# A two-block transformer kernel on one core: rotary exchange by a VectorE shuffle, boundary tiles in PSUM, first loads from two engines

## The chip, the core and the metric

The kernel runs on one core of a Trainium2 chip. The metric is the device time of one launch in microseconds (us), the median of several runs. TensorE multiplies matrices into PSUM; VectorE (DVE), ScalarE (ACT) and GpSimd (POOL) work element by element; SyncE (SP) and ScalarE issue the DMA transfers here. Each engine works off its own instruction stream in order and waits for semaphores of the others.

## What is computed

Two blocks of two layers each on x of 1024 tokens x 1024 columns, in float32. A layer of the first block:

```python
def rotate(x, cos, sin):
    x1, x2 = jnp.split(x, 2, axis=-1)
    return jnp.concatenate([x1 * cos - x2 * sin, x2 * cos + x1 * sin], axis=-1)
...
    h = rms_norm(x, norm_g)
    proj = h @ w_in
    (aq, ak, av, az, cx, cb, cc, cz, rq, rk, rv, rz, gates) = jnp.split(proj, split_points, axis=-1)
    a = diff_attention(aq, ak, av, lam, attn_subln_g, lam_init) * jax.nn.silu(az)
    c = short_conv(cx, cb, cc, conv_w) * jax.nn.silu(cz)
    r = retention(rq, rk, rv) * jax.nn.silu(rz)
    g = jax.nn.sigmoid(gates.astype(jnp.float32)).reshape(b, s, N_BRANCH, D_MODEL)
    merged = g[:, :, 0] * (branches[0] @ w_branch[0])
    ...
    return x + (merged @ w_out).astype(x.dtype)
```

(arguments shortened to what matters). In diff_attention the first 16 of each head's 64 columns of q and k are rotated (two halves of 8 are exchanged and multiplied by the sine); in retention all 64 are (two halves of 32). The first block ends in a further rms_norm. A layer of the second block is again x + y @ w_out, with h = rms_norm(x) ahead of its projection; its y joins a 31-tap convolution, an attention of eight heads and a gated unit, each with a norm of its own.

## The kernel before

Everything is laid out with features on the 128 partitions and tokens along the free axis: X is eight tiles (j) of 128 features x 1024 tokens, worked in two halves of 512 tokens. A product in float32 is made of three: the input is split into a high part (Hhi) and the rest (Hlo), and so is each weight panel (Whi, Wlo, split by GpSimd at L449 and L452 from what SyncE loads at L429); `three_pass` (L502) and `three_pass_half` (L483) issue the 24 matmuls of a half panel. GpSimd splits the next panel once TensorE says `panel_begun`.

All orders are written out by hand, one stream for each engine; nothing is scheduled by a planner. In the first block (`first_block`, L531; TensorE's stream from L688, ScalarE's from L975, VectorE's from L1256) a layer runs: attention over four heads, merge 0, convolution, merge 1, retention in two pairs of heads, merge 2, and 16 output panels OUT (two halves x eight tiles).

The attention of a head has eight queries q of 128 tokens: TensorE's `scores` (L731, with the mask at L736), VectorE's `maxima` (L1274), ScalarE's exponentials (L994), VectorE's `mix` (L1283 to L1285, adds `mixed`), TensorE's transposes of the mixed rows (L709, they wait for `mixed`), and products with the values. TensorE issues the scores of query q+2 before the transposes of q+1. Between the queries the table B1_SLOTS places the pieces of the next head: panel halves `q`, `k`, `v`, `z`, and `sq`/`sk`, a matmul with a permutation matrix (L765, `swapa`) that exchanges the halves of q or k. ScalarE copies the raw panel to SBUF (L1004), TensorE swaps it into another bank of the ring F (three banks), and VectorE multiplies by sine (L1294) and cosine (L1295) and adds (L1297). In retention the same is done over 1024 tokens, with `swapr` at L703.

At a passage between layers VectorE adds each OUT panel to x (L1600; `x_ready`), ScalarE squares it and stores x to the buffer xs, VectorE adds the squares up (`add_out_square`, L1507, and L1512 for the additional norm), TensorE sums them over partitions with a matrix of ones (L684; L673 and L677 in the last layer), ScalarE makes the root (`norm_root`), VectorE scales x (L1452, or L1459 for the second block), ScalarE copies the high part (L1153), VectorE subtracts to get the low one (L1466). The first half of tokens is done during outputs 10 to 15 of the second half, at places that HIGH_AT lists; the second half after the last OUT. OUT uses four banks of PSUM. The second block has the same chain with its own lines (L1770, L2306, L2311, L2429), the MLA branch's `final` scalings and `low` splits among the outputs 3 to 7, and, at its beginning, the panels g and a with the 31 taps on VectorE (L2334), 62 instructions over 1024 columns.

At the start ScalarE issues the loads of x, tables and parameters (L1161, L659 to L664, L1759 to L1761), then squares each of eight token tiles; VectorE scales them (L1435), TensorE turns them (L709), and ScalarE and VectorE split them.

## Time and profile before

| | |
|---|---|
| median of 3 runs | 3921.5 us (3919.44 to 3929.78) |
| the profiled execution | 3918.32 us, its span 3916.4 us |
| TensorE busy | 3709.7 us, 95% |
| VectorE busy | 1857.9 us, 47% |
| GpSimd busy | 1421.8 us, 36% |
| ScalarE busy | 1110.0 us, 28% |
| granted TensorE clock, mean | 0.981 of full speed |

The profile has one row for each group of instructions with their start and length, and behind a row in brackets how long the engine had been idle and which instruction of another engine released it. Idle time of TensorE is what counts first; idle time of the others counts where TensorE waits for them. Matmuls overlap in the pipeline, so the distance between the starts of two rows tells more than a row's length.

### The profile page before, as it was taken

How to read it: one execution, taken by the hardware profiler on the slowest of the kernel's cores; microseconds unless marked ns; L12 is line 12 of the kernel's file. 1: busy time of each engine (PE TensorE's matmuls, PEld its weight loads, DVE VectorE, ACT ScalarE, POOL GpSimd, SP SyncE). 2: the span in 40 equal slices, each digit the busy share in tenths (PEclk: the TensorE clock that was granted, in tenths of full speed). 3: DMA queues.
4: the chain of work that ended last, by engine and by line, in shares of the span. 5: the costliest groups of instructions: out<-in, count | busy, mean ns of one | idle time of the engine just before them, and what ended most of it. 6: DMA issues, size and time to landing. Idle time of an engine off the chain costs nothing.

```text
span 3916.4 us, 43068 instructions
## 1 busy us (share of the span) xinstructions
PE 3709.7 (95%) x16664; PEld 2834.0 (72%) x16664; DVE 1857.9 (47%) x2125; ACT 1110.0 (28%) x1817; POOL 1421.8 (36%) x734
## 2 busy tenths in 40 slices
PE   6989999999999999999999998899899989999998
PEld 5666788887877666788887876777666668766666
DVE  3665113223157555113223148962666589345654
ACT  3334100112212334210112212123465321335542
POOL 1212344432356222344342356433322345333324
PEclk9999999999999999999999998999899989999999
DMA  4000111111133100111111123211111231111122
GB/s 148 28 27 27 51 51 46 44 51 33 36 121 108 33 27 27 46 51 46 48 46 34 40 81 94 93 43 33 33 32 31 94 98 49 33 33 33 32 71 86
DMA packets 75580, 209.40 MB, mean 53 GB/s; under 512 B 9120, under 2 KB 14496, under 8 KB 74912
## 3 DMA queue, kind: packets, MB, share of 16 engines
q1 hardware_dynamic: 52992, 156.98, 13.8%
q10 hardware_dynamic: 22432, 50.18, 3.4%
q8 instruction: 118, 1.93, 0.2%
q14 instruction: 38, 0.31, 0.0%
HBM read 186.16 MB, written 20.97 MB: 53 GB/s over the span
## 4 chain that ended last, share of the span: by engine, by line
PE 85%; DVE 9%; ACT 4%; issue 1%; ACTq 1%; DMA 0%; DVEq 0%
PE psA L502 45%; PE psT L483 16%; PE psA L483 5%; PE psA L1820 3%; PE psA L731 2%; PE psT L1885 2%; PE psT L781 2%; PE psT L1791 1%; PE psT L1796 1%; DVE b_rowmax L1274 1%; DVE Hlo L2311 1%; PE psT L1864 1%; ACT X L994 1%; PE psT L1861 1%; PE psT L703 1%
## 5 line engine op out<-in xcount | busy, mean ns | idle before, releaser
L449 POOL TENSOR_TENSOR Whi<-stage,credit 128x1024 fp32r<-128x1024 f32 (+2 forms) x364 | 605.5, 1664 | 2446.9 <-PE psA L502 1213.2
L452 POOL TENSOR_TENSOR Wlo<-stage,Whi 128x1024 fp32r<-128x1024 f32 (+2 forms) x364 | 815.9, 2242 | 28.5
L502 PE MATMUL psA<-Hhi,Whi 128*128 128x512 f32 x2240 | 703.7, 395 | 11.9 <-ACT b_wk L2054 11.9
L502 PE MATMUL psA<-Hlo,Whi 128*128 128x512 f32 x2240 | 691.1, 390 | 0.0
L502 PE MATMUL psA<-Hhi,Wlo 128*128 128x512 f32 x2240 | 690.8, 390 | 0.0
L502 PEld LDWEIGHTS psA<-Hhi,Whi 128*128 128x128 f32 x2240 | 420.1, 188 | 113.0 <-issue 28.1
L502 PEld LDWEIGHTS psA<-Hlo,Whi 128*128 128x128 f32 x2240 | 421.1, 188 | 88.4
L502 PEld LDWEIGHTS psA<-Hhi,Wlo 128*128 128x128 f32 x2240 | 421.1, 188 | 88.2
L483 PE MATMUL psT<-Hhi,Whi 128*128 128x512 f32 x1024 | 424.8, 415 | 35.0 <-ACT b_upad L1017 18.8
L483 PE MATMUL psT<-Hhi,Wlo 128*128 128x512 f32 x1024 | 404.4, 395 | 0.0
L483 PE MATMUL psT<-Hlo,Whi 128*128 128x512 f32 x1024 | 404.1, 395 | 0.0
L483 PEld LDWEIGHTS psT<-Hhi,Whi 128*128 128x128 f32 x1024 | 196.1, 192 | 92.0 <-issue 52.6
L2334 DVE SCALAR_TENSOR_TENSOR b_wk<-b_ypad,b_cur,b_wk 128x1024 f32<-128x1024 f32 x120 | 227.3, 1895 | 4.1
L483 PEld LDWEIGHTS psT<-Hhi,Wlo 128*128 128x128 f32 x1024 | 195.3, 191 | 43.2
L483 PEld LDWEIGHTS psT<-Hlo,Whi 128*128 128x128 f32 x1024 | 196.2, 192 | 39.1 <-issue 3.4
L483 PE MATMUL psA<-Hhi,Whi 128*128 128x512 f32 x448 | 186.7, 417 | 29.2 <-DVE Hlo L2311 15.3
L483 PE MATMUL psA<-Hlo,Whi 128*128 128x512 f32 x448 | 178.9, 399 | 0.0
L483 PE MATMUL psA<-Hhi,Wlo 128*128 128x512 f32 x448 | 178.4, 398 | 0.0
L1274 DVE TENSOR_REDUCE b_rowmax<-psA 128x1 f32<-128x256 f32 (+7 forms) x128 | 97.0, 757 | 169.4 <-PE psA L736 167.2
L987 ACT ACTIVATE b_wk<-psA 128x1024 f32<-128x1024 f32 x44 | 45.2, 1028 | 443.0 <-PE psA L502 442.9
L1094 ACT ACTIVATE b_wk<-psA 128x1024 f32<-128x1024 f32 x32 | 32.9, 1027 | 440.8 <-PE psA L502 440.8
L1820 PE MATMUL psA<-b_wk 128*128 128x512 f32 (+3 forms) x384 | 149.6, 499 | 5.0 <-ACT b_wk L2075 4.5
(301 smaller groups left out, 4996.9 us busy)
## 6 DMA issues: line engine op xcount, KB each, us to landing
stage<-in_w SPq DMA_DIRECT2D x232, 512.0 KB, 3.5
stage<-in_w SPq DMA_DIRECT2D x68, 256.0 KB, 2.6
xs<-X ACTq DMA_DIRECT2D x64, 256.0 KB, 3.2
stage<-in_w SPq DMA_DIRECT2D x32, 384.0 KB, 3.1
b_wk<-xs ACTq DMA_DIRECT2D x36, 256.0 KB, 4.9
b_wk<-in_x ACTq DMA_DIRECT2D x8, 512.0 KB, 11.3
rope<-in_ropes ACTq DMA_DIRECT2D x4, 1024.0 KB, 7.2
stage<-in_w SPq DMA_DIRECT2D x32, 128.0 KB, 2.1
```

Of the source, the lines that this page charges most:

```text
L449: pool.tensor_tensor(Whi[:, b, 0:n], stage[:, b, 0:n], credit[:, 0:1].broadcast_to([P, n]), ALU.add).then_inc(s.w_hi, 1)
L452: pool.tensor_tensor(Wlo[:, b, 0:n], stage[:, b, 0:n], Whi[:, b, 0:n].bitcast(F32), ALU.subtract).then_inc(s.w_split, 1)
L483: mm = pe.matmul(dst[0:M], w[:, cols], r[k][:, c], start=k == 0 and w is whi and r is rhi, stop=k == nk - 1 and end)
L502: mm = pe.matmul(dst[h], w[:, cols], r[k][:, h * HALF:(h + 1) * HALF], start=first and k == order[0] and r is rhi and w is whi, stop=last ...
L703: mm = pe.matmul(dst[:, c], lhsT, rhs[:, c], start=start, stop=stop)
L731: pe.matmul(dst[:, k0:k1], AQ[h % 2][rows, q * P:n], AK[h % 2][rows, k0:k1], start=True, stop=k1 < n)
L781: mm = pe.matmul(psAV[:, c0:], AVAL[h % 2][:, k * P:(k + 1) * P], WT[:, k, c0:], start=k == 0, stop=k == 4 * g + 3)
L987: act.activation(dst, psA[:, A.buf(use)], func).then_inc(A.freed(use), 1)
L1274: step(dve.reduce_max(rowmax[:, c:c + 1], psA[:, A.buf(use), 0:n], AX_X))
L1820: pe.matmul(dst[:, k0:k1], Q[sd][:, q * P:n], keys[g][:, 0:k1 - k0], start=True, stop=k1 < n)
L1885: mm = pe.matmul(psAV[side_rows(sd), c0:], v[:, b * M_V:(b + 1) * M_V], WT[sd][:, k, c0:], start=k == 0, stop=k == 4 * g + 3)
L2334: ins = dve.scalar_tensor_tensor(out=YC[:, t], in0=ypad[:, t, k:k + SEQ], scalar=col(C2.conv_w + 2 * k + t), in1=YC[:, t], op0=ALU.mult, o ...
```

## The change

Three parts.

1. In the first block the swap matmuls are gone, with the two matrices and ScalarE's copies. VectorE reads the raw panel from PSUM: a stream shuffle with a list of 32 lanes writes the exchanged panel to SBUF, a product takes the raw panel by cosine, and the bank is then free. Retention's columns are permuted on the host (PAIRED), so that its exchange lies within 32 lanes too. `sq` and `sk` are gone from the slots.
2. At the passages the squares, the roots and the scaled tiles lie in PSUM. OUT of the first block uses two banks. The scalings are spread otherwise (NORM_AT, NORM_AT2 in place of HIGH_AT); in the second block the sum comes one output earlier, and `final` is spread over outputs 3 to 6. The last scaling of the first block's output is split: half 0 at outputs 14 and 15, half 1 (`last_finished`) inside the second block, behind its first `glu`. xs is stored by one transfer of 2 MB for each half in place of eight.
3. At the start SyncE issues the first four token tiles, ScalarE only the gains and the other four; rope, parameters and tables come later. The order of turns and panels is another.

The core of the diff:

```diff
-B1_PRELUDE = [("q", 0, 0), ("k", 0, 0), ("sq", 0, 0), ("sk", 0, 0), ("q", 0, 1), ("k", 0, 1), ("sq", 0, 1),
-              ("sk", 0, 1), ("v", 0, 0), ("v", 0, 1)]
+B1_PRELUDE = [("q", 0, 0), ("k", 0, 0), ("q", 0, 1), ("k", 0, 1), ("v", 0, 0), ("v", 0, 1)]
 B1_SLOTS = [([("vt", 0, 0)], [("q", 1, 0), ("x0", 0, 0, True)]),
             ([("vt", 0, 1)], [("q", 1, 1), ("x0", 0, 1, True)]),
-            ([("sq", 1, 0)], [("k", 1, 0), ("b0", 0, 0, True), ("ss", -1, 1)]),
-            ([], [("sq", 1, 1), ("k", 1, 1), ("b0", 0, 1, True)]),
-            ([("sk", 1, 0)], [("z", 0, 0)]),
-            ([("sk", 1, 1)], [("z", 0, 1)]),
+            ([], [("k", 1, 0), ("b0", 0, 0, True), ("ss", -1, 1)]),
+            ([], [("k", 1, 1), ("b0", 0, 1, True)]),
+            ([], [("z", 0, 0)]),
+            ([], [("z", 0, 1)]),
...
+def exchange(half):
+
+    return [i ^ half if i < 2 * half else i for i in range(32)]
+
+
 OUTS = [(half, j) for half in (0, 1) for j in range(KT)]
-HIGH_AT = {10: (0,), 11: (1,), 12: (2, 3), 13: (4,), 14: (5, 6), 15: (7,)}
+NORM_AT = {10: (0, 1), 11: (2, 3), 12: (4, 5), 13: (6, 7)}
+NORM_AT2 = {9: (0,), 10: (1,), 11: (2,), 12: (3,), 13: (4,), 14: (5,), 15: (6, 7)}
...
+        OUT, RSTD, ROOT2 = [psA[:, b, 0:HALF] for b in (0, 1)], psT[:, 1, HALF:], psT[:, 1, 0:HALF]
+        SQ, SQ2, MEAN2, ROOT1 = (psT[:, 1, 0:HALF], psT[:, 0, 0:HALF]), psT[:, 0, HALF:], rraw[:, 0, 0:HALF], rraw[:, 0, HALF:]
+
+        def scaled_tile(L, half, t):
+
+            if L == DEPTH and half:
+                return psT[:, 0, cols(t % 2)]
+            return psA[:, t % 2, HALF:]
...
+            sp.dma_start(ident[:], env.consts[:, K.ident:K.ident + P]).then_inc(consts_in, 16)
+            for t in range(4):
+                sp.dma_start(XT[t], x_tiles[t]).then_inc(x_in[t], 16)
+            for k, dst in ((K.ones, ones[:]), (K.mask, MASK)):
                 sp.dma_start(dst, env.consts[:, k:k + P]).then_inc(consts_in, 16)
...
+                        turn_normed((4, 5))
+                    elif L == 0 and use == ("k", 0, 0):
+                        turn_normed((6, 7))
+                        turn_tokens(0)
+                    elif L == 0 and use == ("q", 0, 1):
+                        turn_tokens(1)
...
-                swap(L, ("swaprq", 0), ("rq", 0), swapr, R_RAWQ)
-                swap(L, ("swaprk", 0), ("rk", 0), swapr, R_RAWK)
...
-                    if n >= 4:
-                        pe.wait_ge(*x_ready.upto(L, n - 3))
-                    elif n % 2 == 0:
-                        pe.wait_ge(*A.drained(L, ("branch", 2, KT - 2 + n // 2)))
-                    three_pass_half(pe, out_bank(psA, n), env.Whi[:, p % 2], env.Wlo[:, p % 2],
+                    if n >= 2:
+                        pe.wait_ge(*x_ready.upto(L, n - 1))
+                    else:
+                        pe.wait_ge(*A.drained(L, ("branch", 2, KT - 2 + n)))
+                    three_pass_half(pe, OUT[n % 2], env.Whi[:, p % 2], env.Wlo[:, p % 2],
...
-                    if L + 1 < DEPTH:
-                        act.dma_start(xs_v[:, j, c], x).then_inc(saved[half].sem, 16)
+                    if L + 1 < DEPTH and j == KT - 1:
+                        act.dma_start(xs_v[:, :, c], X[:, :, c]).then_inc(saved[half].sem, 16)
...
+                step(dve.stream_shuffle(R_ROT, raw, exchange(16)))
+                dve.tensor_tensor(dst, raw, rope[:, 0], ALU.mult).then_inc(A.freed(use), 1)
+                step(dve.tensor_tensor(R_ROT, R_ROT, rope[:, 1], ALU.mult))
+                dve.wait_ge(*A.drained(L, use))
                 dve.tensor_tensor(dst, dst, R_ROT, ALU.add).then_inc(done, 1)
...
+                if kind in ("q", "k"):
+                    dst = (AQ if kind == "q" else AK)[h % 2][:, c]
                     dve.wait_ge(*F.filled(L, use))
-                    dve.tensor_tensor(ROT, psF, rope[:, 1, c], ALU.mult).then_inc(F.freed(use), 1)
-                    step(dve.tensor_tensor(dst, dst, rope[:, 0, c], ALU.mult))
+                    step(dve.stream_shuffle(ROT, psF, exchange(8)))
+                    dve.tensor_tensor(dst, psF, rope[:, 0, c], ALU.mult).then_inc(F.freed(use), 1)
+                    step(dve.tensor_tensor(ROT, ROT, rope[:, 1, c], ALU.mult))
                     dve.wait_ge(*F.drained(L, use))
                     dve.tensor_tensor(dst, dst, ROT, ALU.add).then_inc(rotated.sem, 1)
...
+                if half * KT + t >= 2:
+                    dve.wait_ge(*h_lo.upto(L, half * KT + t - 1))
+                if t == 0:
+                    dve.wait_ge(*((both, half + 1) if L == DEPTH else rstd.upto(L - 1, half + 1)))
+                gain, root = (env.gg, MEAN2) if L == DEPTH else (cur[:, C1.norm:C1.norm + KT], RSTD)
+                dve.scalar_tensor_tensor(out=scaled_tile(L, half, t), in0=X[:, t, cols(half)], scalar=gain[:, t:t + 1],
+                                         in1=root, op0=ALU.mult, op1=ALU.mult).then_inc(h_scaled.sem, 1)
...
+                dve.tensor_tensor(SQSUM[:, c], SQ[L], SQSUM[:, c], ALU.add).then_inc(sq_added.sem, 1)
...
-                    normed(L + 1, 0, HIGH_AT.get(n, ()))
-                    if n == 2 * KT - 2 and L + 1 == DEPTH:
+                    normed(L + 1, 0, NORM_AT.get(n, ()))
+                    if n >= 2 * KT - 2 and L + 1 == DEPTH:
                         for t in range(4):
-                            finished(0, t)
+                            finished(0, n % 2 * 4 + t)
...
+        def last_finished(dve):
+            for j in range(KT):
+                dve.scalar_tensor_tensor(out=X[:, j, cols(1)], in0=X[:, j, cols(1)], scalar=fing[:, j:j + 1], in1=RSTD,
+                                         op0=ALU.mult, op1=ALU.mult).then_inc(x_fin, 1)
...
+        SQ, RSTD, M_ROOT = bank_of((last + 1) % 3), bank_of((last + 2) % 3), psAV
+        HT, MT, OUT_BANKS = [bank_of(last), psAV], [bank_of(last), RSTD], [psA[:, b, cols(h)] for h in (0, 1) for b in (0, 1)]
...
-                        if n == KT + 1:
+                        if n == KT:
...
+                    if 3 <= n < 7:
+                        final(L, 1, n - 3)
+                    if 4 <= n < 8:
                         low(L, 1, n - 4)
```

Three places, as the streams stand. First TensorE in the first head's attention, from the scores of query 4 (512 and 128 columns) to the next panel, before:

```order
L731 MATMUL psA<-b_wk 128x512 [waits b1A1_drained,b1A0_drained]
L731 MATMUL psA<-b_wk 128x512
L731 MATMUL psA<-b_wk 128x128 x2
L736 MATMUL psA<-maskb,identb 128x128 x2
L709 MATMUL psT<-ident,X 128x128 [waits b1F1_drained,b1_mixed]
L709 MATMUL psT<-ident,X 128x128 x3
L765 MATMUL psT<-b_wk,b_swapa 128x512 [waits b1F2_drained,b1F0_drained]
```

and with the change:

```order
L720 MATMUL psA<-b_wk 128x512 [waits b1A1_drained,b1A0_drained]
L720 MATMUL psA<-b_wk 128x512
L720 MATMUL psA<-b_wk 128x128 x2
L725 MATMUL psA<-maskb,identb 128x128 x2
L704 MATMUL psT<-ident,X 128x128 [waits b1F2_drained,b1_mixed]
L704 MATMUL psT<-ident,X 128x128 x3
```

The swap (L765) behind the transposes is gone; the transposes, which wait for `b1_mixed`, follow the scores at once in both.

Second VectorE at the same place, from the maxima of query 3 to the mixing of query 3, before:

```order
L1275 TENSOR_SCALAR b_negmax<-b_rowmax 128x2 [waits b1_dve_step]
L1294 TENSOR_TENSOR b_upad<-psT,rope 128x512 [waits b1F_filled]
L1295 TENSOR_TENSOR b_wk<-b_wk,rope 128x512
L1297 TENSOR_TENSOR b_wk<-b_wk,b_upad 128x512 [waits b1F1_drained,b1_dve_step]
L1283 RECIPROCAL b_inv<-b_rowsum 128x2 [waits b1A1_drained,b1A0_drained,b1_rotated]
L1284 TENSOR_SCALAR X<-X,b_inv,b_lam 128x512 [waits b1_dve_step]
L1285 SCALAR_TENSOR_TENSOR X<-X,b_inv 128x512 [waits b1_dve_step]
```

and with the change (L1276 is the shuffle; what it waits for is the panel's own filling, where before it was the swap's):

```order
L1257 TENSOR_SCALAR b_negmax<-b_rowmax 128x2 [waits b1_dve_step]
L1276 STREAM_SHUFFLE b_upad<-psT 128x512 [waits b1F_filled]
L1277 TENSOR_TENSOR b_wk<-psT,rope 128x512 [waits b1_dve_step]
L1278 TENSOR_TENSOR b_upad<-b_upad,rope 128x512
L1280 TENSOR_TENSOR b_wk<-b_wk,b_upad 128x512 [waits b1F1_drained,b1_dve_step]
L1265 RECIPROCAL b_inv<-b_rowsum 128x2 [waits b1A1_drained,b1A0_drained,b1_rotated]
L1266 TENSOR_SCALAR X<-X,b_inv,b_lam 128x512 [waits b1_dve_step]
L1267 SCALAR_TENSOR_TENSOR X<-X,b_inv 128x512 [waits b1_dve_step]
```

Four instructions, two of them reading the panel in PSUM, now stand between the filling and the mixing, where three stood behind the swap.

Third VectorE at the passage inside the first block, around the last two outputs (L1600 before and L1574 after add an output to x), before:

```order
L1600 TENSOR_TENSOR X<-psA,b_wk 128x512 [waits b1_x_back7,out_filled]
L1507 TENSOR_TENSOR b_wk<-b_wk 128x512 [waits sq_done,sq_added]
L1452 SCALAR_TENSOR_TENSOR X<-X,b_cur,b_wk 128x512
L1466 TENSOR_TENSOR Hlo<-X,Hhi 128x512 [waits h_hi] x2
L1507 TENSOR_TENSOR b_wk<-b_wk 128x512 [waits sq_done,sq_added]
L1452 SCALAR_TENSOR_TENSOR X<-X,b_cur,b_wk 128x512 [waits saved1,rstd]
L1452 SCALAR_TENSOR_TENSOR X<-X,b_cur,b_wk 128x512
```

and with the change (psA and psT are PSUM):

```order
L1574 TENSOR_TENSOR X<-psA,b_wk 128x512 [waits b1_x_back6,out_filled]
L1487 TENSOR_TENSOR b_wk<-psT,b_wk 128x512 [waits sq_done,sq_added]
L1574 TENSOR_TENSOR X<-psA,b_wk 128x512 [waits b1_x_back7,out_filled]
L1487 TENSOR_TENSOR b_wk<-psT,b_wk 128x512 [waits sq_done,sq_added] x2
L1442 SCALAR_TENSOR_TENSOR psA<-X,b_cur,psT 128x512 [waits rstd,h_lo]
L1442 SCALAR_TENSOR_TENSOR psA<-X,b_cur,psT 128x512 [waits h_lo]
L1448 TENSOR_TENSOR Hlo<-psA,Hhi 128x512 [waits h_hi]
```

The scalings and splits that stood between the last two outputs now stand ahead of them, and the store is no longer waited for.

## Rows read from the trace of the kernel before

**Rows 1.** The page: busy times of the engines; engines' shares of the chain.
```profile
PE 3709.7 (95%) x16664; PEld 2834.0 (72%) x16664; DVE 1857.9 (47%) x2125; ACT 1110.0 (28%) x1817; POOL 1421.8 (36%) x734
...
PE 85%; DVE 9%; ACT 4%; issue 1%; ACTq 1%; DMA 0%; DVEq 0%
```

**Rows 2.** Timeline of TensorE, first block's attention: start us, duration us, engine line, [wait <-releaser].
```profile
189.40 1.13 PE L731 MATMUL psA<-b_wk 64*128 64x512 f32 x4
...
190.59 1.08 PE L765 MATMUL psT<-b_wk,b_swapa 128*128 128x512 f32 x2
...
204.12 0.47 PE L483 MATMUL psT<-Hhi,Whi 128*128 128x512 f32 x1 [2.99 <-ACT b_upad L1017]
...
225.66 0.47 PE L483 MATMUL psT<-Hhi,Whi 128*128 128x512 f32 x1 [1.57 <-DVE b_upad L1294]
```

**Rows 3.** Timeline of VectorE, same stretch.
```profile
194.79 2.77 DVE L1297 TENSOR_TENSOR b_wk<-b_wk,b_upad 128x512 f32<-128x512 f32 x1
...
197.79 0.55 DVE L1284 TENSOR_SCALAR X<-X,b_inv,b_lam 128x512 f32<-128x512 f32 x1
...
198.37 0.75 DVE L1285 SCALAR_TENSOR_TENSOR X<-X,b_inv 128x512 f32<-128x512 f32 x1
...
206.06 0.68 DVE L1294 TENSOR_TENSOR b_upad<-psT,rope 128x512 f32<-128x512 f32 x1
...
207.38 0.69 DVE L1297 TENSOR_TENSOR b_wk<-b_wk,b_upad 128x512 f32<-128x512 f32 x1
```

**Rows 4.** Timeline of TensorE, retention's first swaps.
```profile
847.90 1.88 PE L703 MATMUL psT<-b_rraw,b_swapr 128*128 128x512 f32 x4
...
849.62 1.88 PE L703 MATMUL psT<-b_wk,b_swapr 128*128 128x512 f32 x4
```

**Rows 5.** Timeline of the start: ScalarE's queue and TensorE.
```profile
15.42 2.48 ACTq L1761 DMA_DIRECT2D b_causal<-in_consts  x1
...
22.47 1.94 PE L709 MATMUL psA<-ident,b_rtab 128*128 128x128 f32 x8 [22.47 <-DVE b_rtab L1435]
...
55.55 1.97 PE L709 MATMUL psA<-ident,b_rtab 128*128 128x128 f32 x8 [6.41 <-DVE b_rtab L1435]
...
95.12 0.49 PE L731 MATMUL psA<-b_wk 64*128 64x128 f32 x4
```

**Rows 6.** Stretches: window us, length, TensorE's busy us (instructions), granted clock, DMA share, GB/s.
```profile
1230.70:1279.20 48.50, 39.70 (x157) 0.89 0.18 54
2415.90:2473.40 57.50, 29.05 (x104) 0.75 0.35 118
3115.80:3210.10 94.30, 76.01 (x297) 0.87 0.33 107
3862.50:3885.00 22.50, 18.48 (x67) 0.86 0.27 83
```

**Rows 7.** Timeline of TensorE, waits at the three passages.
```profile
1242.38 2.07 PE L684 MATMUL psT<-b_wk,ones 128*128 128x512 f32 x2 [8.80 <-DVE b_wk L1507]
...
2436.24 2.07 PE L673 MATMUL psT<-b_wk,ones 128*128 128x512 f32 x2 [9.85 <-DVE b_wk L1507]
...
2473.40 1.19 PE L502 MATMUL psA<-Hhi,Whi 128*128 128x512 f32 x2 [11.89 <-ACT b_wk L2054]
...
3187.45 2.08 PE L1770 MATMUL psT<-b_wk,ones 128*128 128x512 f32 x2 [5.87 <-DVE b_wk L2429]
```

**Rows 8.** Timeline of VectorE, passage inside the first block.
```profile
1228.08 2.89 DVE L1452 SCALAR_TENSOR_TENSOR X<-X,b_cur,b_wk 128x512 f32<-128x512 f32 x1
...
1239.61 0.74 DVE L1452 SCALAR_TENSOR_TENSOR X<-X,b_cur,b_wk 128x512 f32<-128x512 f32 x1
```

**Rows 9.** Stretches around two waits of TensorE, columns as in rows 6.
```profile
198.00:206.00 8.00, 5.01 (x25) 1.00 0.22 66
2806.00:2812.00 6.00, 4.64 (x11) 0.56 0.23 66
```

**Rows 10.** Stretch of taps: window, length, busy PE PEld DVE ACT POOL, clock, DMA.
```profile
2474.00:2607.00 133.00, 133.00 (x577) 109.82 (x576) 120.25 (x66) 16.58 (x16) 64.79 (x24) 0.98 0.16 48
```

More of the change, by code:

```diff
@@ L682, in sums @@
             if half:
-                pe.wait_ge(*rstd.upto(L - 1, 1))
-            pe.matmul(SUM, ones[:], SQSUM[:, cols(half)], start=True, stop=True).then_inc(summed.sem, 1)
+                pe.wait_ge(*h_scaled.upto(L - 1, KT))
+            pe.matmul(RSTD, ones[:], SQSUM[:, cols(half)], start=True, stop=True).then_inc(summed.sem, 1)
         env.last_sums = last_sums
@@ L710, in turn @@
                 return mm
-            def swap(L, use, raw, mat, raw_tile):
-                pe.wait_ge(*A.drained(L, raw))
-                if T.before(use):
-                    pe.wait_ge(*T.room(L, use))
-                full(psT[:, T.buf(use)], mat[:], raw_tile).then_inc(T.filled_sem, 1)
             def scores(L, h, q):
@@ L1768, in sums @@
             if half:
-                pe.wait_ge(*rstd.upto(L + 1, 1))
-            pe.matmul(SUM, ones[:], SQSUM[:, cols(half)], start=True, stop=True).then_inc(summed.sem, 1)
+                pe.wait_ge(*h_scaled.upto(L + 1, KT))
+            else:
+                pe.wait_ge(*y_lo.upto(L - 1, 12))
+            pe.matmul(RSTD, ones[:], SQSUM[:, cols(half)], start=True, stop=True).then_inc(summed.sem, 1)
         def tensor(pe):
@@ L2189, in scalar @@
             for L in range(DEPTH):
+                if L:
+                    norm_root(L, 1)
+                    for t in range(KT):
+                        h_high(L, 1, t)
+                take(L, ("g", 0), YC[:, 0], ACT.Sigmoid)
                 act.dma_start(pww, env.pww[L]).then_inc(layer_in.sem, 16)
```

344 lines of the change are left out of this document (144 added, 200 removed).

## The prediction, made before the changed kernel ran

> **What bounds the kernel now.** I read the page's shares first: TensorE is busy 3709.7 of 3916.4 us and carries 85% of the chain that ended last [rows 1]. So an edit is worth what it takes from TensorE's own stream, or from the waits of TensorE; about 207 us of the span are such waits. Then I read TensorE's waits stage by stage. They stand in four kinds of place: single waits of 1 to 3 us inside the attention of the first block [rows 2], the start [rows 5], the three passages from one layer to the next and the end [rows 6, 7]. The panel stretches in between have no waits; the change leaves their matmuls alone, and I cost them at nothing. The profiled execution took 3918.3 us; the sum is made against that, and the median of the runs lies 3.2 us above it. About 0.3% (12 us) is what a measurement of this kernel can tell from no change.
>
> **Retention.** The change removes eight swap groups (four in each layer). The two shown start 1.72 us apart [rows 4], and nothing else runs on TensorE meanwhile: 8 x 1.72 = 13.8 us less. What is late next: the second head's sum of squares stood behind one of these swaps and now waits for ScalarE's Square. That wait can't exceed the cover that was taken away, 1.72 us, nor be below nothing; I take 1.25, nearer to the cover, twice: +2.5. Net **-11.3**.
>
> **Attention of the first block, what goes.** Three of the four heads prepare the next head's q and k in slots 0 to 3: four pieces each, so 24 in two layers. Each swap is one three-part matmul group; the one at 190.59 lets the next work start 0.91 us later [rows 2]. 24 x 0.91 = 21.9 us less. Beside it go old waits: the 2.99 us wait for ScalarE at 204.12, seen twice in a layer, and the 1.57 us wait for VectorE at 225.66, seen three times in a layer [rows 2]; both come from buffers of the small ring that the swap results held. 2 x (2 x 2.99 + 3 x 1.57) = 21.4 less.
>
> **Attention, what comes.** Before, VectorE's part of a piece began a whole panel after the raw panel was ready, because a swap stood between; there was slack. Now VectorE's stream says: wait for the panel, shuffle, two products, sum, and only behind these the mixing of the next query, for whose result TensorE's transposes wait. TensorE's stream puts between the panel's last matmul and those transposes only one query's scores. No row shows a shuffle. The nearest are 128x512 operations with one operand in PSUM, 0.68 us, and with both in SBUF, 0.69 alone and 2.77 when GpSimd splits a weight panel at the same time [rows 3]. I take 0.7, since it reads PSUM; the bounds are 0.6 and 1.4. So a piece costs 0.1 of semaphore and 4 x 0.7 = 2.9 us, and the mixing of a 512 wide query another 0.55 + 0.75, with its reciprocal and gaps 1.55 [rows 3]; 256, 384 and 640 wide ones by the same rate 1.15, 1.35 and 1.8. TensorE has 1.2 us of scores in that time (189.40 to 190.59) [rows 2]. By slot:
> slot 0: 2.9 + 1.15 - 1.4 (scores and the value transposes) = 2.65
> slot 1: 2.9 + 1.35 - 1.2 = 3.05
> slot 2: 2.9 + 1.55 - 1.2 = 3.25; in heads 1 and 2 a sum of squares stands in between as well: about 2.3
> slot 3: 2.9 + 1.8 - 3.8 (scores and the first head's value products) = 0.9; in heads 1 and 2 about 2.1, as VectorE arrives late from slot 2.
> That is 9.9 for head 0 and 10.1 for heads 1 and 2: 30 a layer, **+61** in two (rounded up for the semaphores). Half of the SBUF products could meet GpSimd's split, but the split begins with the panel's first half and the piece comes behind its end, so I take 0.69 and not 2.77; if they met, 24 x 2 = +48. Net for attention: -21.9 - 21.4 + 61 = **+17.7**. The fewest that the waits can come to is nothing, if VectorE's mixing were early anyway: then -43.
>
> The row shows 2.77 us for a product of two SBUF operands beside GpSimd's splitting and 0.69 without it, and about 0.68 for one that reads PSUM [rows 3]. The Trainium skill, "SBUF — State Buffer", section "Who interferes with whom", says that a VectorE instruction with at most one SBUF input doesn't contend with GpSimd, while one with two SBUF inputs does: the trace agrees. By that rule the boundary edits below, which move an operand of most 512 wide operations into PSUM, gain what I count for them. The skill's "VectorE: DVE Perf Modes", section "The perf-mode tier table", gives a stream shuffle about 2400 ns for 2048 elements; a quarter of that, an estimate, is 0.6 us; with it the waits would come to 24 x 0.1 = 2.4 us less.
>
> **Start.** ScalarE issues transfers until 17.9 us (its last begins at 15.42 and takes 2.48) [rows 5], and only then squares the first tile. With four of the x tiles on SyncE and the tables later, the first Square is bound by the arrival of x: about 14 us, 5 sooner. The 22.47 us wait at the first transposes and the 6.41 at 55.55 [rows 5] are for VectorE's scaled tiles; the new order puts a panel between pairs of them, and the token copies behind the panels instead of ahead of the first. Together I put the first scores at 77.5 instead of 95.12 [rows 5]: **-17.6**; bounds -8 (only the issue time and the wait at 55.55) and -24.
> Against this part speaks the skill's "DMA: Bandwidth & Descriptors", section "Issuing engines are not separate DMA queues": transfers of several engines interleave on the same 16 DMA engines, and issuing from two saves only the issue time. By it alone the start would gain just the issue, some 5 us of the 17.6, and the total would be 12 us later.
>
> **Layer 0 to layer 1, first block.** 48.5 us between the last output panel and the first scores, 39.70 of them busy [rows 6], with one wait of 8.80 us for the square sums [rows 7]. VectorE was behind there: 2.89 us for one scaling beside GpSimd, 0.74 without [rows 8]. Square, root and scaled tile in PSUM take the contention away, and the single scalings are spread over outputs 10 to 13. Four swaps go (3.8), the half rate that follows the wait goes (about 2.3): 39.7 - 3.8 - 2.3 + 1.3 of waits left = 34.9: **-13.6**.
>
> **First to second block.** 57.5 us, 29.05 busy [rows 6]; waits of 9.85 and 11.89 [rows 7]. The granted clock is 0.75 there [rows 6], so some 4 us of the busy time are half rate. New: 25 + 6 for the chain of sums, roots and first tiles = 31, -26.5; the half rate behind the last wait another -2.8; the two output banks instead of four cost +1.3: **-28**. VectorE's last eight final scalings now stand between glu and the taps of the second block, 8 x 0.7 = 5.6; VectorE is busy for 120.25 of the 133 us of that stretch [rows 10], so there is room for them and they are costed at nothing; without it they would cost these 5.6.
>
> **Layer 0 to 1, second block.** 94.3 us, 76.01 busy, clock 0.87 [rows 6], waits of 5.87 [rows 7] and four shorter. Full rate for all of it gives 68.7; the sum one output earlier waits 1.6, the second half's 3.4: 73.7, **-20.5**. **End.** 22.5 us with 18.48 busy [rows 6]: the four idle us and the half rate behind them (3) go, as the four scalings are spread: **-7**.
>
> **Sum.** -11.3 + 17.7 - 17.6 - 13.6 - 28 - 20.5 - 7 = -80.3: 3838 us for a profiled execution, about **3840** for the median.
>
> **The rivals.**
> *The clock falls at the new waits.* Around a short wait of TensorE at 2807 the granted clock read 0.56 in the mean, thus partly the lower level of 1.2 GHz; after the 2.99 us wait at 204 it stayed at 1.00 [rows 9]. If the first holds for the 24 new waits, each costs about 2 us more: +48, so 3888. Against it: all of the attention of block one keeps 1.00 now.
> *Slower.* The same place, with a higher price: if each piece's wait drops the following panel half (5.5 us at full rate) to 1.2 GHz, that is up to 5.6 us each, 134 in all: 3974. It turns the sum slower from 80/24 = 3.3 us more for each wait on. Nothing in the trace shows a panel wholly at the low clock behind 3 us of waiting.
> *The boundaries give half.* They end in chains of two or three engines that hand on one tile at a time; PSUM shortens the operations, not the semaphores, and two output banks leave less lead. Half of 69 us is +35: 3875. For it: ScalarE's and VectorE's steps of 0.7 us alternate strictly there.
> *The new waits don't appear*, the swaps go for nothing: 3838 - 61 = 3777, about 3779 for the median. That would be so if scores and mixing slid apart by a query; the streams as written don't allow it.
>
> **How the numbers follow.** Forecast 3840: 0.60. Clock falls: 0.14. Half at the boundaries: 0.14. No new waits: 0.07. Slower: 0.04; the last 0.01 is no change. The range takes in the first three with the bounds of the start (+10), the shuffle (24 x 0.7 = +17 at 1.4 us) and, below, half of the fourth: 3808 to 3892. Faster than 3909.7: 0.94; within 0.3%: 0.02; slower: 0.04.
>
> **What would show it.** In the profile after: no swap rows; 24 waits of TensorE's transposes for the mixing, 2 to 3.3 us each, some 60 in all, in the first block's attention; VectorE's shuffle at about 0.7; granted clock 1.00 there. First scores near 77.5. Boundaries of about 35, 31 and 74 us. Wrong is the prediction if these waits are under 30 or over 110 us in all, if the shuffle takes over 1.4, or if a boundary keeps a wait over 7 us.

## The result, and the profile after

The changed kernel takes 3861.2 us (median of 4 runs, 3857.83 to 3863.83), the one before 3922.6 beside it on the same chip: a ratio of 0.984, 95% interval 0.983 to 0.986. The prediction was 3840, range 3808 to 3892. So the direction and the range held, and a part of the forecast gain did not come: -61.4 us by the medians where 81.5 were forecast, and -55.5 us of span between the two profiled executions (3916.4 to 3860.9) where the sum said -80. All stage lengths below are of the profiled executions.

The page of the changed kernel, the lines that answer to [rows 1]:

```profile
PE 3675.3 (95%) x16568; PEld 2822.7 (73%) x16568; DVE 1752.0 (45%) x2205; ACT 1080.9 (28%) x1779; POOL 1398.4 (36%) x734
...
PE 85%; DVE 10%; ACT 3%; issue 1%; DMA 0%; POOL 0%; SPq 0%; ACTq 0%; DVEq 0%; POOLq 0%
```

TensorE is still 95% busy and still 85% of the chain. It lost 34 us of busy time, though the matmuls that are gone were worth about 43 (24 swaps of 0.91 in the attention, 8 of 1.72 in retention, 8 of about 0.95 at the layers' beginnings): some of what stayed has become slower. That is the first hint.

TensorE's waits, kernel after (engine, line <- releaser: us in total, times, longest):

```profile
PE psT L704 <- DVE X L1267: 55.2, 30, 3.0
...
PE psA L704 <- DVE b_rtab L1425: 21.6, 2, 20.7
...
PE psT L668 <- DVE b_wk L1487: 5.4, 1, 5.4
```

The first line is the new wait that the prediction named: 55.2 us, forecast 61. The third is what is left of the 9.85 us of [rows 7].

To see where the time went I took the same instruction in both traces and subtracted its starts. By stage:

| stage | forecast | measured | where in the traces |
|---|---|---|---|
| start to first scores | -17.6 | -11.4 | 95.12 -> 83.72 |
| attention, layer 0 | +8.9 | +17.6 | length 300.5 -> 318.1 |
| attention, layer 1 | +8.9 | +19.0 | 290.5 -> 309.5 |
| retention, both layers | -11.3 | -11.5 | -5.75 and -5.76 |
| layer 0 to 1, first block | -13.6 | -13.8 | 48.5 -> 34.7 |
| first to second block | -28 | -26.2 | 57.5 -> 33.5, and 2 behind it |
| layer 0 to 1, second block | -20.5 | -19.6 | 94.1 -> 74.5 |
| end | -7 | -7.8 | 22.5 -> 14.7 |
| all else | 0 | -1.8 | |
| sum | -80.3 | -55.5 | |

The four stretches that answer to [rows 6], kernel after (window, length, TensorE's busy us, granted clock, DMA share, GB/s):

```profile
1231.60:1266.30 34.70, 34.08 (x147) 1.00 0.38 122
2416.70:2450.20 33.50, 26.93 (x102) 0.90 0.31 100
3090.00:3164.50 74.50, 70.46 (x297) 0.98 0.42 136
3814.70:3829.40 14.70, 14.70 (x67) 1.00 0.29 93
```

The passage inside the first block is now 34.08 of 34.70 us busy at clock 1.00, where it was 39.70 of 48.50 at 0.89; the end has no wait left. The passage to the second block keeps 6.6 us of waits and a clock of 0.90. Nothing there went other than forecast by more than 2 us. The whole miss is in two rows of the table: the attention (+36.6 instead of +17.7) and the start.

The same kind of place as in [rows 3], VectorE after, from the filling of a q panel to the end of the next mixing, and the transposes of TensorE that wait for it:

```profile
105.47 0.73 DVE L1276 STREAM_SHUFFLE b_upad<-psT 128x512 f32<-128x512 f32 x1
106.24 0.69 DVE L1277 TENSOR_TENSOR b_wk<-psT,rope 128x512 f32<-128x512 f32 x1
106.84 0.68 DVE L1278 TENSOR_TENSOR b_upad<-b_upad,rope 128x512 f32<-128x512 f32 x1
107.56 0.69 DVE L1280 TENSOR_TENSOR b_wk<-b_wk,b_upad 128x512 f32<-128x512 f32 x1
108.29 0.17 DVE L1265 RECIPROCAL b_inv<-b_rowsum 128x2 f32<-128x2 f32 x1
108.49 0.48 DVE L1266 TENSOR_SCALAR X<-X,b_inv,b_lam 128x384 f32<-128x384 f32 x1
109.00 0.62 DVE L1267 SCALAR_TENSOR_TENSOR X<-X,b_inv 128x384 f32<-128x384 f32 x1
...
109.67 0.90 PE L704 MATMUL psT<-ident,X 128*128 128x128 f32 x3 [2.97 <-DVE X L1267]
```

The shuffle takes 0.73 us, between the bounds and near the 0.7 that was taken; piece and mixing together run from 105.47 to 109.62, 4.15 us (forecast 2.9 + 1.35), and TensorE stands for 2.97 of them (forecast 3.05).

### The profile page after: what moved, and what is told of

It reads as the page before. It is cut to its first block, busy times and chain, and to the rows that moved or that the text cites. A ratio compares the mean times of both kernels' runs of the same rounds, so it can differ in the third digit from the quotient of the medians.

```text
span 3860.9 us, 42859 instructions
## 1 busy us (share of the span) xinstructions
PE 3675.3 (95%) x16568; PEld 2822.7 (73%) x16568; DVE 1752.0 (45%) x2205; ACT 1080.9 (28%) x1779; POOL 1398.4 (36%) x734
## 4 chain that ended last, share of the span: by engine, by line
PE 85%; DVE 10%; ACT 3%; issue 1%; DMA 0%; POOL 0%; SPq 0%; ACTq 0%; DVEq 0%; POOLq 0%
PE psA L498 45%; PE psT L479 17%; PE psA L479 7%; PE psA L1802 3%; PE psT L1869 2%; PE psT L1773 1%; PE psT L1778 1%; PE psT L768 1%; PE psA L720 1%; PE psT L704 1%; PE psT L1846 1%; PE psT L1843 1%; ACT X L977 1%; DVE b_rowmax L1256 1%; DVE Hlo L2297 1%
## 5 line engine op out<-in xcount | busy, mean ns | idle before, releaser
L448 POOL TENSOR_TENSOR Wlo<-stage,Whi 128x1024 fp32r<-128x1024 f32 (+2 forms) x364 | 798.0, 2192 | 28.5
L977 ACT ACTIVATE X<-psA,b_negmax 128x256 f32<-128x256 f32 (+7 forms) x128 | 93.8, 737 | 338.6 <-DVE b_negmax L1257 338.6
```

What stands on the lines that cost most here:

```text
L448: pool.tensor_tensor(Wlo[:, b, 0:n], stage[:, b, 0:n], Whi[:, b, 0:n].bitcast(F32), ALU.subtract).then_inc(s.w_split, 1)
L977: act.activation(PR[q % 2][c][:, 0:n], psA[:, A.buf(use), 0:n], ACT.Exp, bias=negmax[:, q % 2, c:c + 1], scale=SCALE, accum_out=rowsum[:, ...
```

## The experiments

Each is an edit of the changed kernel; nothing is left out of the computation in any of them.

**1. All of the piece behind the mixing.** VectorE mixes the next query first, then takes its maxima, and only then rotates q or k.

```diff
                         mix(L, h, q)
+                        if q == 4:
+                            for use in later:
+                                piece(L, use, 0)
                         if q + 1 < NT:
                             maxima(L, h, q + 1)
...
+                        for use in later:
+                            piece(L, use, 1 if q == 4 else None)
+                        later = []
...
+                                elif use[0] in ("q", "k"):
+                                    later.append(use)
```

> Edit of the changed kernel: VectorE does the q and k pieces of the next head behind the mixing and the maxima of the next query (in slot 4 the shuffle and first product ahead of the maxima), nothing else. Theory A (the 55.2 us of TensorE waiting for the mixing, L1267, come from the piece standing ahead of the mixing; the 51 us of half clock in the first block's attention come from those waits): the waits fall below 10 us, the granted clock of both attention stretches reads 1.00, time 3861 - 50 - 24 = about 3787. Rival B (the clock falls for another reason, for example because the swaps no longer fill TensorE's stream): waits fall below 10 us but the clock stays near 0.96, time about 3810. Rival C (VectorE's later maxima make as long a wait at the exponentials and the ring of banks): time within 10 us of 3861.

Measured: 3827.1 us (3821.13 to 3831.18), 34 less. Its waits:

```profile
PE psT L479 <- DVE b_wk L1278: 25.3, 11, 2.9
...
PE psT L704 <- DVE X L1267: 2.3, 8, 0.6
```

The wait for the mixing is gone (2.3 us left), but 25.3 us in 11 waits stand at the next panel: it needs a bank of the three-bank ring that the piece, now later, has not emptied. So A is right on what made the 55 us, and part of C is right too. The time is none of those that the three theories gave: A and B had the waits below 10 us in all, C had no gain. The clock, in the windows of the two attentions (before, after, this run):

```profile
95.10:395.60 300.50, 278.41 (x1288) 1.00 0.10 28
1279.20:1569.60 290.40, 269.32 (x1244) 1.00 0.10 28
```

```profile
83.70:401.80 318.10, 279.31 (x1264) 0.96 0.10 28
1266.30:1575.80 309.50, 272.04 (x1222) 0.96 0.09 26
```

```profile
82.80:385.10 302.30, 277.53 (x1263) 0.97 0.10 30
1248.00:1535.10 287.10, 263.64 (x1222) 0.98 0.10 28
```

Before it reads 1.00 (2.4 GHz throughout), after 0.96 in both layers, thus for about 8% of the time the lower level of 1.2 GHz. With the waits fewer, but as long (up to 2.9 us), it reads 0.97 and 0.98.

Shorter windows show where the clock is lost (window, length, TensorE's busy us, clock, DMA, GB/s; the changed kernel). The first is around the wait of 2.97 us at 109.67; the second holds waits of 2.54, 2.97 and 2.09 us for the mixing:

```profile
106.00:116.00 10.00, 7.03 (x24) 0.66 0.00 0
126.00:266.00 140.00, 124.29 (x576) 1.00 0.09 26
```

So the lower clock stands beside long waits, but not beside each of them; in the kernel before, the four waits of 2.98 to 2.99 us in the attention left it at 1.00.

**2. Half of the piece ahead.** Shuffle and first product (which frees the bank) stay ahead of the mixing, sine product and sum follow it.

```diff
                         mix(L, h, q)
+                        for use in later:
+                            piece(L, use, 1)
+                        later = []
...
+                                elif use[0] in ("q", "k"):
+                                    piece(L, use, 0)
+                                    later.append(use)
```

> Edit of the changed kernel: of each q or k piece only the shuffle and the first product stay ahead of the next mixing, the sine product and the sum follow it. Theory A: each of the 24 waits gets shorter by 1.4 us, so TensorE waits 55 - 34 = 21 us for L1267; if the clock falls by the length of the waits it is back at 1.00, which gives 24 more: about 3803; if it falls by their mere number, only 3827. Rival B (clock falls without regard to the waits): 3827 with a clock of 0.96.

Measured: 3826.1 us (3820.31 to 3827.76). Waits and clock:

```profile
PE psT L704 <- DVE X L1267: 27.4, 28, 1.5
...
PE psA L720 <- ACT X L977: 10.3, 6, 2.5
```

```profile
82.50:382.40 299.90, 272.78 (x1264) 0.99 0.10 30
1249.30:1538.30 289.00, 262.32 (x1220) 0.99 0.10 28
```

28 waits for the mixing now, each at most 1.5 us, and the clock is at 0.99 in both layers. This run has more waits than experiment 1 and about the same sum, 27.4 against 25.3, and yet the higher clock. So what the clock goes by here is the length of the single wait more than the number or the sum of the waits, and not the absence of the swaps, since none of these kernels has any. Rival B is out. The time is worse than the 3803 that theory A gave: the waits fell by 27.8 and not 34, the wait for the exponentials (second line) rose from 4.9 to 10.3, and the busy time of the two stretches fell from 551.35 to 535.11 us, 16 of the 25 that the clock had cost.

**3. Mixing first, then the bank, then the maxima.** Mix, shuffle and first product, maxima, sine product and sum.

```diff
                         mix(L, h, q)
+                        for use in later:
+                            if q in (1, 2, 3, 4):
+                                piece(L, use, 0)
                         if q + 1 < NT:
                             maxima(L, h, q + 1)
...
+                        for use in later:
+                            piece(L, use, 1 if q in (1, 2, 3, 4) else None)
+                        later = []
```

> Edit of the changed kernel: in all of slots 0 to 3 VectorE mixes the next query first, then does the shuffle and first product of the piece, then the maxima, then the rest. The all-late order left 25.3 us in 11 waits of 2.2 to 2.9 for a bank of the ring, the half-ahead order 27.4 us in 28 waits of up to 1.5 for the mixing. Theory A2 (the bank is needed about 0.6 us behind the mixing, so these 11 waits shrink to about 1 us each, and waits so short don't bring the clock down): about 12 us of waits, clock 0.99 to 1.00 in the attention, 3826 - 15 - 3 = about 3808. Rival C2 (the maxima, 1.4 us later, make the exponentials late): new waits of over 10 us for the mixing, time 3820 or more.

Measured: 3793.4 us (3791.24 to 3793.70), ratio to before 0.967 (0.966 to 0.969); run again beside others on another chip 3797.3.

```profile
PE psT L479 <- DVE b_wk L1278: 4.4, 9, 0.5
...
PE psT L704 <- DVE X L1267: 2.8, 12, 0.3
```

```profile
83.30:368.00 284.70, 270.17 (x1263) 0.99 0.11 32
1234.20:1508.40 274.20, 260.97 (x1220) 0.99 0.10 29
```

7.2 us of these waits are left, none over 0.5 us, and the two attentions take 284.7 and 274.2 us where the changed kernel takes 318.1 and 309.5: 68.7 us less. The bank waits came out at 0.5 and not 1 us. Compared with the kernel before, the attention now gains 16 us in each layer, 32 of the 43 that the swaps and the old waits were worth in the prediction. Almost all that is left of the lower clock stands at the beginning of a layer, around one wait of 2.46 us for the exponentials (in the kernel before it was 1.94 and 2.24 us long, at a clock of 1.00); layer 0, its first 11.7 us and the rest:

```profile
83.30:95.00 11.70, 9.23 (x43) 0.85 0.29 68
95.00:368.00 273.00, 260.94 (x1222) 1.00 0.10 30
```

C2 is out: the maxima, 1.4 us later, delay nothing; the wait for the exponentials is 4.9 us in all, as in the changed kernel.

**4. Mask and ones loaded first.**

```diff
+            for k, dst in ((K.mask, MASK), (K.ones, ones[:])):
+                sp.dma_start(dst, env.consts[:, k:k + P]).then_inc(consts_in, 16)
             for t in range(4):
                 sp.dma_start(XT[t], x_tiles[t]).then_inc(x_in[t], 16)
-            for k, dst in ((K.ones, ones[:]), (K.mask, MASK)):
-                sp.dma_start(dst, env.consts[:, k:k + P]).then_inc(consts_in, 16)
```

> Edit of the changed kernel: SyncE loads the mask and the ones ahead of the four token tiles, not behind them. Theory D (the first Square at 16.56 us waits for the mask's landing, not for a token tile): first Square at about 10 to 12 us, first panel 2 to 5 us sooner than 34.52, time 3857 to 3859. Rival E (the token tiles, or ScalarE's and VectorE's chain from tile to tile, set the start): first Square sooner but the first panel within 1 us of 34.52, time unchanged.

The start of the changed kernel, then of this run (VectorE's first cast of the mask, ScalarE's first Square, TensorE's first transposes, first panel, first scores):

```profile
16.16 0.23 DVE L1498 CAST maskb<-b_lamt 128x128 bf16<-128x128 f32 x1 [15.24 <-DMA b_lamt<-in_consts]
...
16.56 1.03 ACT L1107 ACTIVATE psT<-b_first 128x1024 f32<-128x1024 f32 x1 [11.28 <-DVE identb L1499]
...
20.70 1.94 PE L704 MATMUL psA<-ident,b_rtab 128*128 128x128 f32 x8 [20.70 <-DVE b_rtab L1425]
...
34.52 0.77 PE L479 MATMUL psT<-Hhi,Whi 128*128 128x512 f32 x1 [2.60 <-DVE Hlo L1432]
...
83.72 0.49 PE L720 MATMUL psA<-b_wk 64*128 64x128 f32 x4
```

```profile
10.61 1.03 ACT L1107 ACTIVATE psT<-b_first 128x1024 f32<-128x1024 f32 x1 [5.57 <-DMA b_first<-in_x]
...
13.85 1.94 PE L704 MATMUL psA<-ident,b_rtab 128*128 128x128 f32 x8 [13.85 <-DVE b_rtab L1425]
...
28.43 0.77 PE L479 MATMUL psT<-Hhi,Whi 128*128 128x512 f32 x1 [2.60 <-DVE Hlo L1432]
```

Measured: 3848.1 us (3846.21 to 3850.79), 13 less. In the changed kernel VectorE had waited 15.24 us for the mask (64 KB behind 2 MB of token tiles), and ScalarE waits for that cast. With the mask first the Square starts at 10.61, released by a token tile, the first panel 6.1 us sooner, and the first scores start at 76.45 in place of 83.72. D holds. About 6 of the 13 us are not at the start; what made them is not shown. A second pair, on another chip, gives 9.3: experiment 3 again, 3797.3, and the same with the mask first, 3788.1.

> The mix-first order in all four slots, with the mask and ones ahead of the token tiles. The version with slot 1 all late gained only 2.2 us over mix-first alone, though its start was 6.8 sooner. If slot 1 had cost the rest, this comes to about 3787; if what the start gains is partly lost again later, it stays at about 3790.

> The mix-first order in all four slots once more, beside the version with the mask first on the same chip: 3793 again, and the difference of the two is the mask's, 6 to 7 us if it all stays.

Measured: 3788.1 (3787.22 to 3793.70) and 3797.3 us (3793.53 to 3799.79). TensorE's first transposes are 6.7 us earlier, the first scores 6.2, the ends 8.4 apart. This is the fastest version, ratio to before 0.966 (0.965 to 0.968). A version with slot 1 wholly late came close to it:

> As the run that mixes first, but where no bank is short (slot 1) the whole piece follows the maxima, and with the mask and ones loaded ahead of the token tiles. If the two gains add: 3808 - 7 at the start = about 3800; if the 6 us that the mask run won beyond the start's own 6.9 were the chance position of its stretches of half clock, no more than that.

Measured: 3791.3 us (3788.90 to 3792.05), less than the 3800 of the expectation because the mixing-first order alone had done better than the 3808 that it was built on. It is 2.2 us below experiment 3 with two edits at once, the mask and the later slot 1, so it does not price the mask. The two pairs that differ in the mask alone do: 13.1 and 9.3 us by the medians, of which 7.3 and 6.2 are there at the first scores.

**5. Squares and root back in SBUF** at the passages of the first block.

```diff
-        SQ, SQ2, MEAN2, ROOT1 = (psT[:, 1, 0:HALF], psT[:, 0, 0:HALF]), psT[:, 0, HALF:], ...
+        SQ, SQ2, MEAN2, ROOT1 = (wk[:, 0, 0:HALF], wk[:, 0, 0:HALF]), wk[:, 1, 0:HALF], ...
+        ROOTS = wk[:, 2, 0:HALF]
```

> Edit of the changed kernel: at both passages out of first block layers the squares, the additional mean and the root (for layer 0 to 1) lie in SBUF again, all else (two output banks, spread, scaled tiles in PSUM) stays. Theory F (the gain of 13 and 26 us at the passages comes from operands in PSUM, which GpSimd's splitting doesn't slow): the additions of squares go back to a mean near 1.8 us in place of 0.7, and the passages lengthen by 5 to 12 us each: 3871 to 3885. Rival G (the gain comes from the order: scalings spread ahead of the last outputs): passages within 2 us, time within 4 us of 3861.

Measured: 3871.6 us (3871.01 to 3872.09), 10.4 more. The additions of squares at the passage to the second block, changed kernel and this one (line engine op, names, shapes, count | busy us, mean ns | idle):

```profile
L1487 DVE TENSOR_TENSOR b_wk<-psT,b_wk 128x512 f32<-128x512 f32 x14 | 9.5, 679 | 0.0
```

```profile
L1488 DVE TENSOR_TENSOR b_wk<-b_wk 128x512 f32<-128x512 f32 x14 | 21.8, 1560 | 0.0
```

679 ns with one operand in PSUM, 1560 ns with both in SBUF (1801 in the same group before). The mean of 1560 hides two kinds: nine of the 14 additions ran beside GpSimd's splitting and took 2.05 us in the mean, five ran without it and took 0.68. With the operand in PSUM, 13 of the 14 ran beside GpSimd and still took 0.68. So it is GpSimd at work that costs the time, and PSUM takes that away. The passage inside the first block got 3.0 us longer and the one to the second block 10.1; elsewhere the profiled run came out 4.8 us shorter, which stays open. F holds as the mechanism, with more of it at the second passage, where there are two sums of squares. The Trainium skill, "SBUF — State Buffer", section "Who interferes with whom", names this pair of cases: two SBUF inputs contend with GpSimd's reads, at most one does not. The runs agree, 2.05 against 0.68 us beside GpSimd.

**6. The old spread of the scalings.**

```diff
-NORM_AT = {10: (0, 1), 11: (2, 3), 12: (4, 5), 13: (6, 7)}
+NORM_AT = {10: (0,), 11: (1,), 12: (2, 3), 13: (4,), 14: (5, 6), 15: (7,)}
```

> Edit of the changed kernel: the first half's scalings at both passages of the first block stand again at the outputs 10 to 15 as before the change (one, one, two, one, two, one) and not two each at 10 to 13; all tiles stay in PSUM. The squares back in SBUF cost 3.0 us at the passage inside the first block and 10.1 at the one to the second block, out of gains of 13 and 26. Theory H (the rest of the gain is the order, which empties VectorE's stream ahead of the last two outputs): the two passages lengthen by 3 to 8 us each, 3867 to 3877. Rival I (the rest is the swaps that are gone and the half clock): within 3 us of 3861.

Measured: 3865.7 us (3861.45 to 3869.53), 4.4 more with ranges that overlap (the changed kernel's runs reach 3863.83). By the starts of the same instructions the passage inside the first block is 0.1 us longer and the one to the second block 2.4. Between 3860.9 and 3867.7, the spans of the two profiled runs, only 2.5 us are at the passages. So the order is worth little once the operands are in PSUM: H, with 3 to 8 us at each passage, falls at both. Rival I's bound, within 3 us of 3861, is passed too, but with overlapping ranges 4.4 us can't be told from nothing.

**7. ScalarE's transfers ahead of the sigmoid.** At the passage to the second block the wait of 11.89 us [rows 7] was for ScalarE's sigmoid (L2054). The trace of before shows what stood ahead of it in ScalarE's queue, 16 stores of x (13.91 us from the first to the end of the last), what VectorE did meanwhile, and when the sigmoid began:

```profile
2453.64 13.91 ACTq L1254 DMA_DIRECT2D xs<-X  x16
...
2454.91 11.82 DVE L1496 SCALAR_TENSOR_TENSOR X<-X,b_fing,b_wk 128x512 f32<-128x512 f32 x12
...
2472.23 1.02 ACT L2054 ACTIVATE b_wk<-psA 128x1024 f32<-128x1024 f32 x1
```

Each store waits for the final scaling of its own tile (`x_fin`). Four tiles had been scaled earlier, and their stores follow each other in 0.4 to 0.5 us; the next twelve start one by one behind VectorE's twelve scalings, of which two took over 2 us beside GpSimd. So the 13.91 us are in part VectorE's time and not ScalarE's for issuing. Behind the stores stood five small loads (3.3 us) and the load of the sigmoid's table (1.28 us). The expectation of the first run below took all of the 13.91 us as issue time.

First eight stores of the first half in place of one, then also the five small loads ahead of the sigmoid:

```diff
-            act.dma_start(xs_v[:, :, cols(0)], X[:, :, cols(0)]).then_inc(saved[0].sem, 16)
+            for j in range(KT):
+                act.dma_start(xs_v[:, j, cols(0)], X[:, j, cols(0)])\
+                    .then_inc(saved[0].sem if j == KT - 1 else env.saved_more, 16)
```

> Edit of the changed kernel: at the passage to the second block the first half of x is stored by eight transfers again instead of one. Before the change ScalarE issued 16 of them (13.91 us) ahead of the sigmoid for which TensorE waited 11.89 us. Theory J (that wait was ScalarE's issue time): seven more transfers at 0.87 us each put the sigmoid 6.1 us later, TensorE waits about 4 to 6 us at the second panel, 3865 to 3868. Rival K (the transfers are issued beside the work): no wait, time unchanged.

Measured: 3859.4 us (3854.71 to 3863.98), no wait: the eight took 4.46 us, 0.56 each and not 0.87, and the sigmoid ended 0.86 us ahead of the panel that needs its bank. The expectation had not counted this slack, and its 0.87 held the waiting for VectorE. The second edit on top of the first:

```diff
-                take(L, ("g", 0), YC[:, 0], ACT.Sigmoid)
+                if L:
+                    take(L, ("g", 0), YC[:, 0], ACT.Sigmoid)
                 act.dma_start(pww, env.pww[L]).then_inc(layer_in.sem, 16)
...
                 if L == 0:
+                    take(L, ("g", 0), YC[:, 0], ACT.Sigmoid)
                     act.wait_ge(env.x_fin, 2 * KT)
```

> The version with eight stores, and ScalarE's first sigmoid of the second block also behind the five small loads. In the run with eight stores the sigmoid ended at 2450.73, 0.86 us ahead of the panel at 2451.59 that needs its bank. Theory J (ScalarE's issue time is the wait, once its slack is used up): the five loads take 3.1 us, so TensorE waits 2 to 2.5 us for the sigmoid at that panel, about 3862. Rival K (issues go on beside the work): no wait.

```profile
2434.61 4.46 ACTq L1235 DMA_DIRECT2D xs<-X  x8
...
2442.43 1.28 ACT L2041 ACT_TABLE_LOAD   x1 [7.23 <-issue]
...
2443.72 1.02 ACT L2041 ACTIVATE b_wk<-psA 128x1024 f32<-128x1024 f32 x1
...
2444.89 1.12 PE L499 MATMUL psA<-Hhi,Whi 128*128 128x512 f32 x2 [2.44 <-ACT b_wk L2041]
```

The wait is there, 2.44 us, in the bounds of 2 to 2.5. The time, 3854.3 us, was taken once and is lower than expected; the row is the evidence, not the time. In the changed kernel J holds: the five loads take 3.3 us, 0.86 of them go into the slack and 2.44 come out as TensorE's wait. For the 11.89 us of before, J is only a part. At 0.56 us each, an estimate from the row of eight, the 16 stores would have taken 9 of the 13.91 us; the other 5 are waiting for VectorE's scalings. The change took both away at once: it moved the scalings, to outputs 14 and 15 and into the second block, and it put one store ahead of the sigmoid in place of 16. No run here separates the two.

## Why the prediction was right, and what it mis-sized

**Attention, what goes.** Right to the tenth for the waits: the wait for ScalarE (L1017, now L999) fell from 18.8 to 6.9 us over the whole span and the one for L1294 from 10.0 to 0.5, 21.4 together, as the term said. The price of a swap was read as that of a group of three matmuls; in the program it is one call, in the trace two rows [rows 2]. The 0.91 us are the distance of two starts and do not depend on that.

**Attention, what comes.** The mechanism and the place were right: 55.2 us less the 1.5 that the same wait had before, 53.7, against +61. There are 30 waits and not 24, because six mixings elsewhere wait 0.2 us each. Slot by slot the 24 were 2.54, 2.97, 2.95 and 0.73 us in head 0 (forecast 2.65, 3.05, 3.25 and 0.9) and 2.54, 2.97, 2.09 and 1.33 in heads 1 and 2 (forecast 2.65, 3.05, 2.3 and 2.1). The two operations with both operands in SBUF seldom met GpSimd's splitting, as forecast: 0.70 and 0.84 us in the mean. So the row sum is -21.9 - 21.4 + 53.7 = +10.4, 7 better than the +17.7.

**The term that was mis-sized** is the clock, which the sum put at nothing and a rival priced apart. Measured is +36.6, so 26 us are neither swaps nor waits. TensorE's busy time in both attentions is 551.35 us where it was 547.73, though 21.9 us of swaps are gone: the rest has become 25.5 us longer. The granted clock of 0.96 over 318.1 and 309.5 us says the same: 4% of each, about 12.5 us, twice. The forecast had set this at 0 with the one row in which a wait of 2.99 us left the clock at 1.00 [rows 9], and the rival had set it at 48. The truth is between, 1.1 us for each of the 24 long waits. Experiments 1 and 2 and the short windows show why one row was no basis: at waits of 2.1 to 3.0 us the clock falls at some and stays at others; among the waits of 1.5 us or less of experiment 2 it fell once. How it is decided for each wait stays open. The total came as near to the forecast as it did partly by luck: the row sum was 7 us better than forecast, and took that much off the 26 of the clock. Of the signs that the prediction named, the clock of 1.00 in the attention and the first scores near 77.5 did not come; the others did.

**Slower.** The mechanism of this rival is that of the clock, with 5.6 us for each wait; it measured 1.1, far from the 3.3 that the prediction gave as the turning point.

**Start.** -11.4 instead of -17.6. The step that failed here is "the first Square is bound by the arrival of x: about 14 us". It began at 16.56, bound by the mask, which the change itself had put behind four tiles on SyncE's queue; the diff of the change shows it, and the prediction had read only the tiles. That is 2.6 of the 6.2. VectorE's first two scalings ran beside GpSimd and took 2.19 and 3.37 us where later ones alone take 1.28, 3.0 more; that these are the rest is argued from the rows, not tested. With the mask first (experiment 4) the first Square starts at 10.61, and the first scores at 76.45, where the term had said 77.5. The Trainium skill, "DMA: Bandwidth & Descriptors", section "Issuing engines are not separate DMA queues", says that issuing from two engines saves only issue time. By it the start would have gained 5 us; it gained 11.4, in which the new order of turns and panels has a part, so this start tells nothing against the rule.

**Retention and the passages.** -11.5 for -11.3; -13.8, -26.2, -19.6 and -7.8 for -13.6, -28, -20.5 and -7. Experiment 5 shows the share of the squares, the additional mean and the root in PSUM, 3.0 and 10.1 us in the first two; experiment 6 that the spread, to which the prediction gave part of it, is worth 0.1 and 2.4. The rest of these gains (the swaps, the scaled tiles in PSUM, the single store, the split final scaling) was not taken apart. The 11.89 us wait before the second block had another cause than the chain of sums and roots to which the prediction put the passage: ScalarE's sigmoid stood behind 16 stores, most of which waited for VectorE's final scalings, and behind five loads (experiment 7). The sum came out right because the wait is gone either way, which is luck. The eight final scalings that moved behind glu were costed at nothing. They took 0.74 us each on VectorE and cost TensorE at most 0.5 us: the panels just before and beside them start 26.0 us sooner than in the kernel before, those behind them 25.5. "The boundaries give half" is out, and so is "the new waits don't appear".

## What to carry to other kernels

When an operation between two engines is taken out, the work behind it moves up in time, onto whatever the receiving engine does next: look at its stream for what is queued behind the moved step and who waits for it, and put that first. Here the same instructions in another order, mixing first, then the two that free the bank, then the maxima, turn a loss of 37 us in the attention into a gain of 32. In this kernel it paid to keep single waits of TensorE short rather than few: 28 waits of at most 1.5 us were cheaper in clock than 11 of up to 2.9. A small constant needs its place in the queue as much as the large tiles do: two loads of 64 KB, moved ahead of 2 MB, brought the first transposes 6.7 us forward. And a long row in a DMA queue is not issue time by itself: look at what each transfer waits for before pricing it.

## What the runs showed of the hardware

A stream shuffle of 128x512 from PSUM to SBUF took 0.73 us, about as much as a product of that size (0.69), with a separate mask load of 0.01 us ahead of it. Issuing stores of 256 KB that waited for nothing held ScalarE's queue for 0.56 us each in a row of eight; one of 2 MB held it for 0.38. An addition of 128x512 with both operands in SBUF took 0.68 us without GpSimd at work and 2.05 in the mean beside it; with one operand in PSUM it took 0.68 either way. The granted clock over 300 us of attention read 1.00, 0.96, 0.97 to 0.98 and 0.99 with waits (TensorE's, for one kind of instruction) of at most 3.0 us seen twice a layer, up to 3.0 seen 15 times a layer, up to 2.9 seen five or six times a layer, and up to 1.5 seen 14 times a layer. In the version that mixes first it reads 1.00 over the 273 us behind the first 11.7 us of layer 0, where no wait is longer than 1.31 us. At the start, with the mask first, the transposes stand apart by waits of up to 2.5 us, and the stretch from 14 to 29 us has a clock of 0.75; the changed kernel has 1.00 there.
